# Stick-breaking products on VectorE, a reordered head of the front region, and a shorter wait before mixing

## What is computed

```python
q, k, v = jnp.split(proj[..., OFF_SB:OFF_GATE], 3, axis=-1)
y_sb = stick_breaking_attention(to_heads(q), to_heads(k), to_heads(v))
# per block of 128 queries, 8 heads of 64:
#   A[t,s] = sig(z_ts) prod_{s<j<t} (1 - sig(z_tj)), s < t strictly;  out = A @ v
y_rwkv = (group_norm(out_of_recurrence) * lnx_w + lnx_b + bonus) * g   # per head of 64 channels
gates = jax.nn.sigmoid(proj[..., OFF_GATE:OFF_RWKV].reshape(b, s, 3, D_MODEL) + gate_b)
branches = jnp.einsum("bsnc,ncd->bsnd", jnp.stack([y_conv, y_sb, y_rwkv], axis=2), branch_proj)
merged = jnp.einsum("bsnd,bsnd->bsd", gates, branches)
return merged @ w_mix_out, v_first
```

## Time and profile before

| what | value |
|---|---|
| median of 3 runs | 2240.03 us |
| profiled execution, its own time | 2237.44 us |
| its span, first to last instruction | 2235.7 us |
| mean granted TensorE clock | 0.959 |
| PE busy | 2079.4 us (93%) |
| PEld busy | 1649.9 us (74%) |
| DVE busy | 1120.9 us (50%) |
| ACT busy | 782.4 us (35%) |
| POOL busy | 152.0 us (7%) |

### The profile page before, as it was taken

How to read it: one execution, slowest core, us unless ns; L and a number is a source line. 1 busy time by engine, 2 the same in 40 slices (tenths; PEclk the granted TensorE clock), 3 DMA queues, 4 the chain that set the end, 5 groups by cost and what they waited for, 6 DMA issues and landing times. The chain is left out here.

```text
span 2235.7 us, 29732 instructions
## 1 busy us (share of the span) xinstructions
PE 2079.4 (93%) x11888; PEld 1649.9 (74%) x11888; DVE 1120.9 (50%) x1714; ACT 782.4 (35%) x1270; POOL 152.0 (7%) x187
## 2 busy tenths in 40 slices
PE   6999775998999999999999989989899899999997
PEld 5888424875887887888888868876566678888886
DVE  4653566437444454567775334314666664433433
ACT  3112433223223343444443222233455544422421
POOL 0000412532000000000000010000000000000000
PEclk9999687999999999999999999978999999999998
DMA  4233100001332241122233423211110122232222
GB/s 152 95 102 96 32 1 1 3 3 63 100 100 91 92 146 64 57 94 94 95 102 103 163 87 108 94 38 29 38 37 31 42 92 93 94 101 97 94 95 84
DMA packets 47853, 173.54 MB, mean 78 GB/s; under 512 B 5144, under 2 KB 7448, under 8 KB 47488
## 3 DMA queue, kind: packets, MB, share of 16 engines
q1 hardware_dynamic: 45440, 162.99, 22.0%
q0 software_dynamic: 1728, 8.23, 1.1%
q10 hardware_dynamic: 576, 0.84, 0.1%
HBM read 169.90 MB, written 2.13 MB: 77 GB/s over the span
## 5 line engine op out<-in xcount | busy, mean ns | idle before, releaser
L207 DVE TENSOR_TENSOR weights_lo<-weights_raw,weights_hi 128x1024 fp32r<-128x1024 f32 (+2 forms) x288 | 363.5, 1262 | 791.2 <-ACT weights_hi L199 791.1
L199 ACT ACTIVATE weights_hi<-weights_raw 128x1024 fp32r<-128x1024 f32 (+2 forms) x288 | 313.5, 1089 | 868.5 <-PE end_ps L232 245.7
L230 PE MATMUL sp_ps<-arena_parts,weights_hi 128*128 128x512 f32 x720 | 283.6, 394 | 3.0 <-DVE arena_parts L291 2.5
L232 PE MATMUL sp_ps<-arena_parts,weights_lo 128*128 128x512 f32 x720 | 281.6, 391 | 0.0
L231 PE MATMUL sp_ps<-arena_parts,weights_hi 128*128 128x512 f32 x720 | 281.5, 391 | 0.0
L230 PE MATMUL end_ps<-arena_parts,weights_hi 128*128 128x512 f32 x576 | 224.8, 390 | 2.2 <-DVE arena_parts L2872 1.7
L232 PE MATMUL end_ps<-arena_parts,weights_lo 128*128 128x512 f32 x576 | 224.1, 389 | 0.0
L231 PE MATMUL end_ps<-arena_parts,weights_hi 128*128 128x512 f32 x576 | 224.1, 389 | 0.0
L230 PE MATMUL fr_ps<-arena_parts,weights_hi 128*128 128x512 f32 (+1 forms) x480 | 183.7, 383 | 15.0 <-DVE arena_parts L293 8.4
L231 PE MATMUL fr_ps<-arena_parts,weights_hi 128*128 128x512 f32 (+1 forms) x480 | 181.8, 379 | 0.0
L232 PE MATMUL fr_ps<-arena_parts,weights_lo 128*128 128x512 f32 (+1 forms) x480 | 181.5, 378 | 0.0
(11 more groups left out here) (382 smaller groups left out, 3178.1 us busy)
## 6 DMA issues: line engine op xcount, KB each, us to landing
weights_raw<-w_up SPq DMA_DIRECT2D x44, 512.0 KB, 3.4
weights_raw<-w_proj SPq DMA_DIRECT2D x38, 512.0 KB, 3.5
weights_raw<-w_gates SPq DMA_DIRECT2D x32, 576.0 KB, 3.7
weights_raw<-w_ca SPq DMA_DIRECT2D x32, 512.0 KB, 3.4
weights_raw<-w_down SPq DMA_DIRECT2D x16, 704.0 KB, 4.1
weights_raw<-w_in SPq DMA_DIRECT2D x22, 512.0 KB, 3.4
weights_raw<-w_logits SPq DMA_DIRECT2D x16, 512.0 KB, 3.4
weights_raw<-w_ff1a SPq DMA_DIRECT2D x16, 512.0 KB, 3.4
```

The costliest lines, as they stand in the source:

```text
L199: act.activation(self.w_hi[:, g % 2, 0:cols], self.raw[:, g % 2, 0:cols], ACT.Copy).then_inc(self.hi_ready, 1)
L207: dve.tensor_tensor(self.w_lo[:, g % 2, 0:cols], self.raw[:, g % 2, 0:cols], self.w_hi[:, g % 2, 0:cols].bitcast(F32), ALU.subtract).then_ ...
L230: pe.matmul(out, left[0], right[0], start=start, stop=False)
L232: return pe.matmul(out, left[1], right[0], start=False, stop=stop)
```

## The change

Stick-breaking stage:
- GpSimd's `last_part` is gone. VectorE's `multiply` makes the products of part 2 too, in two instructions (columns 0 to 255 and 256 to 383), behind the scans of part 2. One semaphore counts all products.
- VectorE takes the output of pair c - 1 behind the products of part 2 of pair c. Before, it did so behind those of part 1, ahead of part 2's scans.

Front region:
- TensorE makes the variance sums directly behind the means, ahead of step 0 (before: ahead of step 4), and spreads the inverse ahead of step 10 (before: step 12).
- GpSimd's queue loses the eight y low parts. VectorE makes the first four behind all x low parts, and y low part 4 + c behind the `finish` of tile c.
- VectorE: x low parts 0 and 1 ahead of the centring, 2 and 3 behind it; `invert` ahead of x low parts 4 to 7; one `shift` behind `variance`, the others one by one ahead of their `finish`.
- ScalarE: four x high parts ahead of the squares and not three, no y high parts between the squares, `root` ahead of the other x high parts, all y high parts behind these.
- Ahead of mixing TensorE waits for `pairs_free` to reach 3·8 + 1 and not 3·8 + 3: for the product of gate 0 of the last d, not for those of gates 1 and 2.

```diff
 def turn(c, m, side):
     h = 2 * c + side
-    if m < 2:
-        pe.wait_ge(att_ready, 4 * c + 2 * m + side + 1)
-    else:
-        pe.wait_ge(last_ready, h + 1)
+    pe.wait_ge(att_ready, 6 * c + 2 * m + side + 1)
...
-                def last_part(c):
-                    for side in range(2):
-                        pool.wait_ge(left, 6 * c + 5 + side)
-                        for lo, hi in ((0, 256), (256, 384)):
-                            ins = pool.tensor_tensor(part(att, side, 2)[:, lo:hi - 1], part(stop, side, 2)[:, lo:hi - 1],
-                                                     part(keep, side, 2)[:, lo + 1:hi], ALU.mult)
-                        ins.then_inc(last_ready, 1)
...
-                    if c and m == 0 and side == 1:
-                        last_part(c - 1)
-                last_part(NW - 1)
...
                     dve.wait_ge(left, at + 1)
-                    dve.tensor_tensor(part(att, h, m)[:, 0:n - 1], part(stop, h, m)[:, 0:n - 1], part(keep, h, m)[:, 1:n], ALU.mult)\
-                       .then_inc(att_ready, 1)
+                    for lo, hi in ((0, n),) if m < 2 else ((0, 256), (256, n)):
+                        ins = dve.tensor_tensor(part(att, h, m)[:, lo:hi - 1], part(stop, h, m)[:, lo:hi - 1], part(keep, h, m)[:, lo + 1:hi],
+                                                ALU.mult)
+                    ins.then_inc(att_ready, 1)
...
                         for side in range(2):
-                            if m < 2:
-                                multiply(c, m, side, 6 * c + 2 * m + side)
-                        if c and m == 1:
-                            take(c - 1)
+                            multiply(c, m, side, 6 * c + 2 * m + side)
+                    if c:
+                        take(c - 1)
...
         to.means(pe)
+        to.variances(pe)
         for m in range(36):
-            if m == 4:
-                to.variances(pe)
-            if m == 12:
+            if m == 10:
                 to.spread_out(pe)
             step(m)
...
-    def gpsimd(self, pool):
-        for k in range(KD):
-            self.y_split.lo(pool, k)
...
-        for k in range(3):
+        for k in range(4):
             self.x_split.hi(act, k)
         for c in range(NW):
             to.take_square(act, c)
-            if c < 2:
-                self.y_split.hi(act, 2 * c)
-                self.y_split.hi(act, 2 * c + 1)
-        for k in range(3, 6):
+        to.root(act)
+        for k in range(4, KD):
             self.x_split.hi(act, k)
-        to.root(act)
-        for k in range(6, KD):
-            self.x_split.hi(act, k)
-        for k in range(4, KD):
+        for k in range(KD):
             self.y_split.hi(act, k)
...
+        for k in range(2):
+            self.x_split.lo(dve, k)
         for c in range(NW):
             to.centre(dve, c)
-        for k in range(4):
+        for k in range(2, 4):
             self.x_split.lo(dve, k)
         to.variance(dve)
-        for k in range(4, 6):
+        to.shift(dve, 0)
+        to.invert(dve)
+        for k in range(4, KD):
             self.x_split.lo(dve, k)
-        to.invert(dve)
-        for k in range(6, KD):
-            self.x_split.lo(dve, k)
-        for c in range(NW):
-            to.shift(dve, c)
+        for k in range(NW):
+            self.y_split.lo(dve, k)
         core.split_lo(dve, g0 + 2)
         for c in range(NW):
+            if c:
+                to.shift(dve, c)
             to.finish(dve, c)
+            self.y_split.lo(dve, NW + c)
             if c:
                 self.r_split.lo(dve, c - 1)
             if c == 1:
                 core.split_lo(dve, g0 + 3)
...
             def _(pool):
-                gates.gpsimd(pool)
                 cross.gpsimd(pool)
...
                 gates.tensor(pe)
-                pe.wait_ge(gates.pairs_free, 3 * KD + 3)
+                pe.wait_ge(gates.pairs_free, 3 * KD + 1)
                 mix.tensor(pe)
```

More of the change, by code:

```diff
@@ L558, in stick_breaking_stage @@
     turned = core.sem("sb_turned")
-    placed, last_ready = core.sem("sb_placed"), core.sem("sb_last_ready")
+    placed = core.sem("sb_placed")
     order = [(c, m, side, 6 * c + 2 * m + side) for c in range(NW) for m in range(3) for side in range(2)]
```

## The result

The changed kernel takes **2223.68 us** (median of 4 runs, 2222.23 to 2225.71) where the kernel before, measured again beside it, takes 2239.57 us. The ratio is 0.9936, with a 95% interval from 0.9921 to 0.9951: 15.9 us or 0.64% faster. Forecast were 10.1 us. The profiled execution took 2223.99 us with a span of 2222.2, which is 13.5 us under the span before. The traces can explain these 13.5 us; the other 2.4 come from which executions were profiled: that of the kernel before lies 2.1 us under its median, that of the changed kernel 0.3 over.

The account below looks back on a forecast made before the run. TensorE, full from 548.1 to 719.8, only passes on what happens ahead, so three local terms add: -4.7 - 1.2 - 4.2 = -10.1 us, from the median 2240.03 to 2229.9 us. The 8-in-10 range was 2223 to 2236.

Parts of the forecast that it names:

- Part 1, ring and tail: Stick-breaking: three ScalarE gaps waiting for GpSimd's product go (-2.84 us) and the last output starts earlier (-1.9): -4.7 us.
- the tail: End of stick-breaking: the last six transposes follow directly, so the last output starts near 300.7 instead of 302.61: 1.9 us.
- The cover: Stick-breaking: VectorE's products, up to 1.4 us a turn, land in its 4.21 us hole waiting for the output.
- the ring itself: Stick-breaking: copies, scores and sigmoids share a bank; ScalarE and TensorE taking turns sets the period, next in line as limit.
- Part 1, clock: Stick-breaking: clock effect taken as 0, range -2.5 to +2 us, one output changing clock being worth 2.0 us.
- Part 2: Head of the front region: new order -3.6 us, clock loss +2.4, together -1.2 us, range -3.6 to +1.2.
- The clock term: Head of the front region: low clock behind the gaps before steps 22 and 23 costs 2.4 us.
- Part 3: Change to mixing: seven steps start behind the last gate, tile 2 at 733.9 against 738.1: -4.2 us.
- B: Clock kept: front gaps don't lower it, stick-breaking outputs at full clock (-2 us for one); 14.5 us, 2225.5; chance 0.17.
- C: Stick-breaking gives nothing: VectorE's queue delays the next pair's scans, or the ring has another late member; 2234.6 us; chance 0.10.
- D: Mixing wait fails: tile 1 held at its weights or the eighth step; sum -6, 2234 us; chance 0.08.
- E: Slower: clock stays at 1.2 GHz through stick-breaking, deciding once its clock is under 0.55; +2.7 us, 2242.7; chance 0.05.

Follow-up runs that it names:

- run 5: The changed kernel as it is, measured once more: 2226.85 us, ratio 0.9943 to the kernel before.
- run 1: The kernel before with the stick-breaking part of the change alone: 2229.66 us, ratio 0.9960.
- run 8: The changed kernel with all eight y low parts made by VectorE in one row, behind the x low parts: 2219.50 us, ratio 0.9922.
- run 3: The kernel before with only the wait ahead of mixing lowered by two: 2233.93 us, ratio 0.9992, in two groups of times.
- run 2: The kernel before with the new order at the head of the front region alone: 2239.32 us, ratio 1.0007.
- run 7: The changed kernel with matmuls whose results nobody reads added in TensorE's idle time of stick-breaking: 2221.48 us, ratio 0.9925.
- run 4: The kernel before with matmuls whose results nobody reads added in TensorE's idle time of stick-breaking: 2231.88 us, ratio 0.9982.
- run 6: The kernel of run 1 with the output taken where it was, ahead of part 2's scans: 2230.76 us, ratio 0.9973.

## Why the prediction was right or wrong

**Part 1, ring and tail: right.** 2.84 us for the gaps against 3.2 measured, 1.9 for the tail against 1.5, 4.7 against 4.7, the last by luck, since the two misses cancel. The cover held: VectorE's four products lie in its idle time, and nothing in the turns waits for them. What I named as next in line, the ring itself, is next. The tail's 0.4 us is a step left out: I took the last products for ready, without following the masks and scans ahead of them. With the third output at 1.2 GHz, as I had assumed, they are ready (run 5: 2.0 us); with it at 2.4 GHz TensorE comes 0.58 us too early.

**Part 1, clock: this is the step that failed.** The prediction took 0 and kept -2.5 to +2. Measured were -6.4. The working priced "one output moved from one clock to the other". All three outputs ahead of the last were slow in the kernel before (3.90, 4.22 and 4.39 us), and so were the scores of part 2 in each turn. The row of 0.69 for the stage says how much there was: some 43 of its 69.0 us at 1.2 GHz, with three outputs, each worth up to 2 us, in them. The direction was seen ("the ring becomes denser, which speaks for the clock if anything"), the bound was not worked out from all the rows that it covered. The gain comes again: the ring took 54.4 us in the trace after and in runs 1 and 8, 55.3 in run 5, where the old stick-breaking took 65.5, 65.4 and 65.3 (before, and runs 3 and 2). Run 7 shows that the clock is worth time in this ring, since more work in it makes it shorter. That the denser ring is what raised the clock is argued from runs 4 and 7, where filling idle time raised it too (0.67 to 0.82 and 0.76 to 0.90); no run made the ring denser in another way.

**Part 2, order of events: right; its sum: wrong in sign in the first trace.** The variance sums start at once behind the means. The gaps before steps 22 and 23 came as told (3.11 and 2.74 us for 3.1 and 2.9), and run 8 shows that they hang on y low parts 6 and 7. The clock term, 2.4 us of loss, was mis-sized: the clock fell on steps 4, 10 and 23 and the means were slow too, which makes most of the 6.1 us over the 45.9 that the forecast has for the head at full clock, so that +2.5 us came out, beyond the +1.2 that the part's own range ended at. The same kernel's second trace gave 48.3, which is -1.2 against 49.5, as forecast. And the old head took 53.5 us in runs 1 and 6. So the head's time with either order is spread by 4 us, by where the low stretches fall; alone (run 2) it changes nothing that can be told.

**Part 3: right**, -4.3 for -4.2, with its two gaps (1.90 and 1.05 us for about 2 and 1.3). Only the extra loss for a low clock (0.3) did not come here, and came, at 0.5, in run 3.

**The rivals.** The result is B's side, 2225.5 and better, but for B's second reason alone: the outputs came to lie at full clock, while the gaps of the front did lower it. B assumed 2.0 us for that and needed 6.4. The Trainium skill (TensorE: Matmul & The Clock Gate, What's actually happening) has the clock fall behind a whole idle window. At 512.6 the trace after shows it falling right behind the spread, whose matmuls of 8 rows follow step 9 and keep TensorE busy, by the profile, for all 4.00 us from 508.3, so that rule does not cover this fall. Nor is the spread enough by itself: in the second trace of the changed kernel and in the kernel before, the steps behind it run at 2.4 GHz. What the same section says of a window that is not tied to the kernel's start, so that the same kernel meets it elsewhere from run to run, agrees with 48.3 and 52.0 us for one and the same head. C is refuted by the trace after and by run 1, whose rings are 11 us shorter with nothing in the turns waiting for VectorE. D is refuted by the trace after. E is refuted by a stage clock of 0.76 against its 0.55.

The range held the time (2223.7 against a lower end of 2223) by little, and that is luck: the clock's terms of parts 1 and 2 were both bounded too closely, and since they went opposite ways they partly made up for each other.

## What to carry to other kernels

Where TensorE waits in short pieces, price the clock apart from the waits: list every instruction that lies on the chain and runs at 1.2 GHz in the trace before, and take what they would gain at 2.4 GHz as the bound of what a denser order can give. Here the three outputs ahead of the last and the scores of part 2 in the three turns would have given an estimate of 5.4 + 2.2 = 7.6 us (from 3.90, 4.22 and 4.39 against 2.37, and three times 1.65 against 0.92); 6.4 came. A mean clock is no price; a low stretch costs only where TensorE is the one that is waited for. And when a step is moved into a row of an in-order engine, look at what the row behind it waits for: two low parts behind one weight group cost about as much as the new order had won (heads of 49.5 before, 50.4 in run 2, 45.5 in run 8).

## What the runs showed of the hardware

- Work that nobody needs can make a kernel faster: 2226.85 to 2221.48 us with ten matmuls more in the stage, at a clock of 0.90 and not 0.73 to 0.76 (run 7 beside run 5).
- With the same instructions, 1497.5 us and 1503.9 us from tile 2 of mixing to the end, and heads of 49.5 and 53.5 us, with the clock as the difference. The changed kernel by itself shows it too: 1496.7 and 1501.9 us, and heads of 52.0 and 48.3 us, in its two traces. Such spreads are as large as the terms of a change of 0.5%, so a part's gain is better read between two marks of a trace than from the medians alone (run 3: 3.8 us between the marks, and an interval from -4.5 to +0.9 us for the whole).
